# Retention with the decay powers folded into the keys, the mask and the normalisation, and with a block-diagonal state

## What is computed

```python
kc = (k * RET_QK_DIM ** -0.5)          # qc, kc, vc: q, k, v in chunks of c tokens
intra_decay = jnp.where(rel >= 0, jnp.exp(log_gamma[:, None, None] * jnp.maximum(rel, 0.0)), 0.0)
s = jnp.einsum('bnchd,bnshd->bnhcs', qc, kc) * intra_decay
intra = jnp.einsum('bnhcs,bnshe->bnche', s, vc)
k_decay = jnp.exp(log_gamma[:, None] * (CHUNK - 1 - pos)[None, :])
kv = jnp.einsum('bnshd,hs,bnshe->bnhde', kc, k_decay, vc)
def step(state, kv_n):
    return state * chunk_decay + kv_n, state
...
q_decay = jnp.exp(log_gamma[:, None] * (pos + 1.0)[None, :])
cross = jnp.einsum('bnchd,hc,bnhde->bnche', qc, q_decay, prev)
o = head_rmsnorm((intra + cross).reshape(B, S, RET_HEADS, RET_V_DIM))
o = jax.nn.silu(g) * o
```

## Time and profile before

| | us |
|---|---|
| median of 3 runs | 2108.87 (2107.14 to 2109.91) |
| span of the profiled execution | 2105.2 |

### The profile page before, as it was taken

The page is one execution under the profiler, slowest core; times in us unless marked ns, Lnnn a source line. Parts: engine busy times, 40 slices in busy tenths (PEclk is TensorE's granted clock), DMA queues, the critical chain, the costliest instruction groups (busy, mean ns, idle before and its releaser), DMA issues. The chain is left out here.

```text
span 2105.2 us, 30095 instructions
## 1 busy us (share of the span) xinstructions
PE 1959.5 (93%) x11159; PEld 1057.1 (50%) x11159; DVE 1599.9 (76%) x1704; ACT 1056.7 (50%) x1396; POOL 545.7 (26%) x347
## 2 busy tenths in 40 slices
PE   6999988989399999999994899959999999999999
PEld 5785446654244454544443555534544444444444
DVE  6866637753799999999987655484697898889876
ACT  6333327731488888888874555484332333332320
POOL 2222130000133333333320001022003665456530
PEclk9999989999699999999997999979999999999999
DMA  6111410051399999999997446437101112121112
GB/s 245 41 41 41 137 33 1 1 213 60 120 376 413 405 411 410 401 400 404 401 363 273 179 149 233 141 112 264 41 1 61 60 41 80 40 80 40 64 56 80
DMA packets 80627, 363.69 MB, mean 173 GB/s; under 512 B 14088, under 2 KB 27528, under 8 KB 47960
## 3 DMA queue, kind: packets, MB, share of 16 engines
q1 hardware_dynamic: 61704, 309.64, 37.5%
q0 software_dynamic: 18832, 52.80, 7.3%
HBM read 337.21 MB, written 37.75 MB: 178 GB/s over the span
## 5 line engine op out<-in xcount | busy, mean ns | idle before, releaser
L649 DVE SCALAR_TENSOR_TENSOR split<-stage,split 128x2048 f16<-128x2048 f32 x128 | 289.6, 2283 | 5.4 <-ACT split L645 3.6
L432 PE MATMUL ps<-split,xt 128*128 128x512 f16 (+1 forms) x776 | 289.7, 373 | 0.6 <-DVE xt L499 0.6
L433 PE MATMUL ps<-split,xt 128*128 128x512 f16 (+1 forms) x776 | 289.6, 373 | 0.0
L434 PE MATMUL ps<-split,xt 128*128 128x512 f16 (+1 forms) x776 | 289.4, 373 | 0.0
L645 ACT ACTIVATE split<-stage 128x2048 f16<-128x2048 f32 x128 | 240.5, 1904 | 94.6 <-PE ps L434 94.6
L1400 POOL TENSOR_TENSOR stage<-stage 128x1024 f32<-128x1024 f32 x48 | 134.1, 2793 | 266.8 <-DVE split L860 263.9
L432 PE MATMUL ps<-xt,split 128*128 128x512 f16 (+1 forms) x528 | 188.9, 358 | 6.9 <-issue 5.2
L433 PE MATMUL ps<-xt,split 128*128 128x512 f16 (+1 forms) x528 | 189.0, 358 | 0.0
L434 PE MATMUL ps<-xt,split 128*128 128x512 f16 (+1 forms) x528 | 188.9, 358 | 0.0
L649 DVE SCALAR_TENSOR_TENSOR arena<-arena 128x2048 f16<-128x2048 f32 x64 | 146.3, 2286 | 3.1 <-ACT arena L645 3.1
L855 ACT ACTIVATE split<-stage 128x1024 f16<-128x1024 f32 x56 | 57.3, 1048 | 143.2 <-PE pt L434 72.9
(11 more groups left out here) (542 smaller groups left out, 4816.2 us busy)
## 6 DMA issues: line engine op xcount, KB each, us to landing
stage<-in_w_gate SPq DMA_DIRECT2D x64, 1024.0 KB, 7.5
stage<-in_w_up SPq DMA_DIRECT2D x64, 1024.0 KB, 7.8
arena<-in_w_down SPq DMA_DIRECT2D x64, 1024.0 KB, 8.3
stage<-in_w_mlp SPq DMA_DIRECT2D x32, 1024.0 KB, 4.9
stage<-in_w_dense_a SPq DMA_DIRECT2D x16, 1024.0 KB, 8.3
arena<-in_conv_taps POOLq DMA_DIRECT2D x22, 640.0 KB, 4.9
stage<-in_w_dense_b SPq DMA_DIRECT2D x12, 1024.0 KB, 12.0
resid<-in_x SPq DMA_DIRECT2D x16, 512.0 KB, 7.0
```

What stands on the lines that cost most here:

```text
L432: nc.tensor.matmul(out_ap, lh, rh, start=start, stop=False)
L433: nc.tensor.matmul(out_ap, lh, rl, start=False, stop=False)
L434: return nc.tensor.matmul(out_ap, ll, rh, start=False, stop=stop)
L649: nc.vector.scalar_tensor_tensor(out=wlo(s), in0=wstage(s), scalar=WS, in1=whi(s), op0=ALU.mult, op1=ALU.subtract).then_inc(s_wo[s], 1)
```

## The change

Write p for a token's place in its block and g for a head's factor. DVE's reads of the keys from PSUM now multiply by g^(127 - p) / 8 in the same instruction (DVE therefore takes the groups 2, 3, 6, 7, ACT 0, 1, 4, 5). The mask becomes g^-128 on and above the diagonal, and the queries' factor g^(p + 1), constant along a row of the output, moves into the normalisation: as a scale per partition (`rdec`) of ACT's Squares, and as one small product on the reciprocal in `mix`. So qd is gone, and ktok is a plain copy, which ACT now makes (`keys_by_token(n)`, ahead of the statistics of block n - 1 in ACT's order). The state keeps both heads of a pair side by side, 128 x 512, each head's other half zero, in two buffers; DVE zeroes the two PT banks once before the loop. The product with the state is then one matmul of 256 columns for two heads, straight from QR. The products of keys and values come before the waits of the outputs, with a semaphore count of their own, and block 7's transposes and state product, which nobody reads, are gone. The constants c_ret shrink from 1536 to 774 columns. The semaphores' declarations change only in name.

```diff
         onesb = half[:, 6 * P:7 * P]
         ret = Z[:, 0:RET_COLS]
         decT = ret[:, 0:512].rearrange("p (b c) -> p b c", b=2)
-        kdec = ret[:, 512:768]
-        qdec = ret[:, 768:1280].rearrange("p (t j c) -> p t j c", t=2, j=2)
-        cdec = ret[:, 1280:1536]
-        pos = Z[:, RET_COLS:RET_COLS + (S + NH * P) // 2].bitcast(F16)
+        kdec = ret[:, 512:768].rearrange("p (t s) -> p t s", t=2)
+        cdec = ret[:, 768:770]
+        rdec = ret[:, 770:774]
+        pos = Z[:, 1536:1536 + (S + NH * P) // 2].bitcast(F16)
         pos_k = pos[:, 0:S]
         pos_q = pos[:, S:S + NH * P].rearrange("p (h q) -> p h q", h=NH)

...
             return PS[:, 2 * m:2 * m + 2, :].rearrange("p b c -> p (b c)")

         sT = [xn[:, 0, 0:512], xn[:, 0, 512:1024]]
-        qd = [xn[:, 1, 0:512], xn[:, 1, 512:1024]]
-        ktok = [junk[:, 256:512], junk[:, 512:768]]
-        state = junk[:, 0:256]
+        ktok = [xn[:, 1, 0:256], xn[:, 1, 256:512]]
+        state = [junk[:, 0:512], junk[:, 512:1024]]
         zero = cols[:, 42:43]
         lam_in = sq
         lam_dot = cols[:, 64:192].rearrange("p (j d) -> p j d", j=2)
...
                 nc.scalar.activation(chunk_dest(0, ft, tk), PS[:, g % 4, :], ACT.Copy, scale=IWS)\
                     .then_inc(s_free[g % 4], 1)

-            for g in (0, 2, 4):
+            for g in (0, 1, 4):
                 read(g)
             token_hi("T2")
             token_hi("T3")
             proj_hi(act, 1, "S4")
             token_hi("T1")
-            read(6)
+            read(5)
             token_hi("T4")
             proj_hi(act, 1, "S3")
             proj_hi(act, 1, "S1")
...
+            def keys_by_token(n):
+                act.wait_ge(s_rsc, n + 1)
+                if n >= 2:
+                    act.wait_ge(s_lam, 1 + n - 1)
+                nc.scalar.activation(ktok[n % 2], PS[:, 2 * (n % 2), 256:512], ACT.Copy).then_inc(s_sig, 1)
+
+            def out_stats(n):
                 act.wait_ge(s_ro, n + 1)
                 if n:
                     act.wait_ge(s_rmix, n)
                 for h in range(NH):
                     i = nc.scalar.activation(gb[:, h * DV:(h + 1) * DV],
                                              PT[:, 2 + n % 2, h * DV:(h + 1) * DV], ACT.Square,
-                                             accum_out=ss4[:, h:h + 1])
+                                             scale=rdec[:, h:h + 1], accum_out=ss4[:, h:h + 1])
                 ch.done(i)
                 nc.scalar.activation(std4, ss4, ACT.Sqrt, bias=eps, scale=1.0 / DV).then_inc(s_rss, 1)
+
+            for n in range(TT + 1):
+                if n < TT - 1:
+                    keys_by_token(n)
+                if n:
+                    out_stats(n - 1)
             seven(3)
             seven(4)
             for n in (14, 15):
...
             def read(g):
                 dve.wait_ge(s_full[g % 4], g // 4 + 1)
                 _, ft, tk = chunk_groups(0)[g]
-                nc.vector.tensor_scalar(chunk_dest(0, ft, tk), PS[:, g % 4, :], IWS, None, ALU.mult)\
-                    .then_inc(s_free[g % 4], 1)
+                by_block = lambda v: v.rearrange("p (b s) -> p b s", b=4)
+                nc.vector.scalar_tensor_tensor(out=by_block(chunk_dest(0, ft, tk)), in0=by_block(PS[:, g % 4, :]),
+                                               scalar=IWS, in1=kdec[:, ft - 2:ft - 1, :].to_broadcast([P, 4, P]),
+                                               op0=ALU.mult, op1=ALU.mult).then_inc(s_free[g % 4], 1)

             def token_lo(name):
                 n = T_SPLITS.index(name) + 1
...
             dve.wait_ge(s_xl, TT)
-            read(1)
+            dve.wait_ge(s_const, 16 * 8)
+            read(2)
             ch.done(nc.vector.tensor_tensor(TF["T1"], XF[:, 0:4, :], XH[:, 0:4, 0:512], ALU.subtract))
             read(3)
             nc.vector.tensor_tensor(TF["T1"], TF["T1"], XL[:, 0:4, 0:512], ALU.subtract).then_inc(s_hs, 1)
             nc.vector.tensor_tensor(TF["T3"], XF[:, 4:8, :], XF[:, 0:4, :], ALU.subtract).then_inc(s_hs, 1)
             dve.wait_ge(s_hs, 1)
             nc.vector.tensor_tensor(TF["T2"], XF[:, 4:8, :], TF["T1"], ALU.subtract).then_inc(s_hs, 1)
-            read(5)
+            read(6)
             token_lo("T2")
             token_lo("T3")
             proj_lo(dve, 1, "S4")
...
             seven(2)

             def masked(n):
-                par, blk = n % 2, slice(n * P, (n + 1) * P)
+                par = n % 2
                 dve.wait_ge(s_rsc, n + 1)
+                if n < TT - 1:
+                    dve.wait_ge(s_sig, 4 + n + 1)
                 if n >= 2:
                     dve.wait_ge(s_ro, n - 1)
                 nc.vector.tensor_tensor(sT[par].rearrange("p (b c) -> p b c", b=2),
-                                        PS[:, 2 * par:2 * par + 2, 0:256], decT, ALU.mult)
-                nc.vector.tensor_tensor(ktok[par], PS[:, 2 * par, 256:512], kdec, ALU.mult)
-                for t in range(2):
-                    i = nc.vector.tensor_tensor(
-                        qd[par][:, t * 256:t * 256 + 256].rearrange("p (j c) -> p j c", j=2),
-                        QR[:, t:t + 1, blk].to_broadcast([P, 2, P]), qdec[:, t, :, :], ALU.mult)
-                i.then_inc(s_rm, 1)
+                                        PS[:, 2 * par:2 * par + 2, 0:256], decT, ALU.mult).then_inc(s_rm, 1)

             def update(n):
-                dve.wait_ge(s_ro, n + 1)
+                dve.wait_ge(s_lam, 1 + n + 1)
                 if n == 0:
-                    nc.vector.tensor_copy(state, PT[:, n % 2, 256:512]).then_inc(s_rst, 1)
+                    nc.vector.tensor_copy(state[1], PT[:, 0, :]).then_inc(s_rst, 1)
                 else:
-                    ch.done(nc.vector.tensor_tensor(state, state, cdec, ALU.mult))
-                    nc.vector.tensor_tensor(state, PT[:, n % 2, 256:512], state, ALU.add).then_inc(s_rst, 1)
+                    dve.wait_ge(s_ro, n)
+                    dve.wait_ge(s_rst, n + 1)
+                    for t in range(2):
+                        c = slice(2 * t * DV, 2 * (t + 1) * DV)
+                        i = nc.vector.scalar_tensor_tensor(
+                            out=state[(n + 1) % 2][:, c], in0=state[n % 2][:, c], scalar=cdec[:, t:t + 1],
+                            in1=PT[:, n % 2, c], op0=ALU.mult, op1=ALU.add)
+                    i.then_inc(s_rst, 1)

             def mix(n):
                 dve.wait_ge(s_rss, n + 1)
                 ch.done(nc.vector.reciprocal(rst4, std4))
+                ch.done(nc.vector.tensor_tensor(rst4, rst4, rdec, ALU.mult))
                 for h in range(NH):
                     hs = slice(h * DV, (h + 1) * DV)
                     i = nc.vector.scalar_tensor_tensor(
...
                         scalar=rst4[:, h:h + 1], in1=SG[:, n, hs], op0=ALU.mult, op1=ALU.mult)
                 i.then_inc(s_rmix, 1)

+            nc.vector.memset(PT[:, 0, :], 0.0)
+            nc.vector.memset(PT[:, 1, :], 0.0).then_inc(s_rst, 1)
             for n in range(TT + 2):
                 if n < TT:
                     masked(n)
-                if 1 <= n <= TT:
+                if 1 <= n < TT:
                     update(n - 1)
                 if n >= 2:
                     mix(n - 2)
...
                     pe.wait_ge(s_rm, n - 1)
                 for h in range(NH):
                     t, r = h // 2, slice(DH * (h % 2), DH * (h % 2) + DH)
-                    nc.tensor.matmul(PS[:, 2 * par + h % 2, t * P:(t + 1) * P], KR[r, t, blk], QR[r, t, blk],
-                                     start=True, stop=True)
-                for t in range(2):
-                    i = nc.tensor.transpose(PS[:, 2 * par, 256 + t * P:384 + t * P], KR[:, t, blk], ident)
+                    i = nc.tensor.matmul(PS[:, 2 * par + h % 2, t * P:(t + 1) * P], KR[r, t, blk], QR[r, t, blk],
+                                         start=True, stop=True)
+                if n < TT - 1:
+                    for t in range(2):
+                        i = nc.tensor.transpose(PS[:, 2 * par, 256 + t * P:384 + t * P], KR[:, t, blk], ident)
                 i.then_inc(s_rsc, 1)

             def outputs(n):
-                par = n % 2
+                par, blk = n % 2, slice(n * P, (n + 1) * P)
+                if n < TT - 1:
+                    pe.wait_ge(s_sig, 4 + n + 1)
+                    pe.wait_ge(s_rst, max(n, 1))
+                    for h in range(NH):
+                        r0 = DH * (h % 2)
+                        i = nc.tensor.matmul(PT[r0:r0 + DH, par, h * DV:(h + 1) * DV], ktok[par][:, h * DH:(h + 1) * DH],
+                                             VR[:, n, h * DV:(h + 1) * DV], start=True, stop=True)
+                    i.then_inc(s_lam, 1)
                 pe.wait_ge(s_rm, n + 1)
                 if n:
-                    pe.wait_ge(s_rst, n)
-                for h in range(NH):
-                    t, r0 = h // 2, DH * (h % 2)
```

(37 more changed lines are left out.)

## The result

The changed kernel took 2113.69 us (median of 9 runs, 2110.03 to 2115.84), the kernel before 2108.47 beside it (9 runs, 2107.14 to 2111.03). The ratio of the runs is 1.0019, 95% interval 1.001 to 1.0028: about 4 us longer (0.0019 x 2108.47), and within the 0.2% (4.2 us) that was called no change. The forecast was 2112.0.

A forecast was written before the change was run, and what follows sets the result against it. Prediction: a DVE-ACT loop through the key copy bounds the retention, PE outside it; start +0.27, middle +3.68, end -0.78 give +3.2 us, on 2108.87 making 2112.0 us; range 2107 to 2116.5.

The forecast's parts named there:

- The loop: Retention: mix, statistics, key copy, mask product, update, mix run in turn, a round of 5.19 us against 4.27, +0.92.
- The terms: Retention round: the single times, such as Squares' surcharge 0.36, copy 0.40, masked 0.60, update 0.80, mix 1.13, summing to 5.19 us.
- Start: Retention's first blocks, with DVE zeroing two banks: outputs(2) starts at 156.46 instead of 156.19, +0.27 us.
- Middle and end: Retention: outputs(3) to outputs(6) add 4 x 0.92 = +3.68 us; outputs(7), without a key copy, gives -0.78.
- The sign that PE idles 1.4 or more a round: Retention: PE idle 1.4 us or more each round, put down to DVE's mix, would show the forecast right.
- Chunk 0: Reads of chunk 0: swapped groups shift T2's low half and weight splits by +3.2 us, 1.5 of cover remains, no cost.
- The total: Whole kernel: +3.2 on a span of 2105.2, plus 3.7 us between span and median, gives 2112.0, called no change.
- The longer loop: Retention rival: same loop but longer, slower from a round of 5.45 us on, up to 2115.5; chance 0.22.
- S2's weights: Chunk 0 rival: a shift over 4.7 us makes PE stall in `seven(3)`'s counterpart `seven(1)`, 2113.6 at 1.5 beyond; chance 0.05.
- The case of low prices: Retention rival: with terms at their lower bounds rounds take 4.54 us, sum -1.1, 2107.8, no change as well; chance 0.15.
- The PE-bound case: Retention rival: key copies not behind the statistics, four rounds of 3.78 us, -4.2 in all, 2104.7; chance 0.08.
- The rival of a fallen clock: Retention rival: PE's clock falls to 1.2 GHz, its 3.78 us doubles to 7.6 and bounds the round, 2122; chance 0.04.

The follow-up runs named there:

- the experiment with the earlier copy: Changed kernel with ACT copying the keys of block n + 1 ahead of the statistics of block n - 1: 2105.08 us, ratio 0.9987.
- the copy twice: Changed kernel with ACT reading the keys once more, into columns nothing uses, just before each key copy behind the statistics: 2109.36 us, one execution.
- early copy, twice: Changed kernel with the key copies one block earlier, ahead of the statistics, and each made twice by ACT: 2103.74 us, one execution.
- PE filled: Changed kernel with five more matmuls of 128 columns in each outputs(n), into a bank nobody reads at the time: 2111.25 us, ratio 1.0017.
- plain Squares: Changed kernel without the scale column on ACT's Squares, so the sums leave out the rows' decay factor: 2112.03 us, ratio 1.0011.
- two statistics buffers: Changed kernel with two buffers for sums, roots and reciprocals, so statistics of block n wait for mix(n - 2): 2105.93 us, ratio 0.9984.
- copy on DVE, two buffers: Changed kernel with DVE copying the keys and two buffers for the statistics: 2103.89 us, ratio 0.9976.

## Why the prediction was right, step by step

- **The loop: right.** mix, statistics, key copy, mask product, update, mix: 5.19 was the sum, 5.21 is measured. All four tests of it (order, engine, buffers, dose) came out on its side.
- **The terms.** The Squares are 0.37 each, as forecast; with their plain form 0.36 a round is gone. The copy starts 0.20 after the Sqrt and takes 0.36 (0.40 taken). The mask product takes 0.61 to the next start (0.60). The two halves of the update take 0.78 to the reciprocal (0.80). Reciprocal 0.21, the small product 0.19 (0.20 each) and mix 1.13. From the copy's end to the mask product it is 0.09, where 0.03 was taken: this and the shorter copy cancel, so that the sum is within 0.02 is in part luck.
- **The Trainium skill on the Squares' scale** (ScalarE: Activation LUTs, What ACT_TABLE_LOAD costs), that a pointer operand adds about 93 ns to an ACTIVATE: the trace agrees, 0.37 against 0.28, and the plain form shortened the whole round by four times that.
- **Start: right.** outputs(2) was expected at 156.46 and came at 156.79, of which 0.25 had come before the retention. The two zeroings:

```profile
147.29 0.48 DVE L2023 MEMSET pt<- 128x512 f32 x1 [0.18 <-DVE arena L1943]
147.84 0.48 DVE L2024 MEMSET pt<- 128x512 f32 x1
```

 0.55 from start to start (0.60 taken), with 0.18 idle ahead. The estimate from the Trainium skill's rule (VectorE: DVE Perf Modes, Zero memsets can be issued as uint32), 0.53 a bank, was 0.02 off the step and 0.05 off the length. What the zeroing costs the kernel by itself wasn't tried.
- **Middle and end: right.** 181.12 - 177.62 = 3.50 from outputs(6) to outputs(7) (3.49 forecast), and 1.89 for the last outputs (1.89). The sign that PE idles 1.4 or more a round held in four of six rounds; in the other two the low clock took the idle time up. `seven(3)` at 183.01 for 182.6; on PE +3.32 for +3.2.
- **Chunk 0: right, and narrow.** DVE's timeline of the changed kernel:

```profile
65.53 0.69 DVE L1900 SCALAR_TENSOR_TENSOR arena<-ps,zone 128x512 f32<-128x512 f32 x1 [4.53 <-PE ps L433]
66.14 4.49 DVE L1907 TENSOR_TENSOR resid<-arena,resid 128x2048 f16<-128x2048 f32 x2
...
81.21 5.76 DVE L570 SCALAR_TENSOR_TENSOR split<-stage,split 128x1024 f16<-128x1024 f32 x5
```

 DVE waits 4.53 us for group 6. T2's low half begins at 66.14 where it was 62.72, 3.4 later, 0.25 of it from before; the splits run from 81.21. The third of the five ends near 81.21 + 3/5 x 5.76 = 84.7, and PE takes S2 at

```profile
86.23 0.27 PE L431 MATMUL ps<-split,resid 128*128 128x256 f16 x1
```

 without a gap: it is busy 64.00 of 64.00 us from 80 to 144. The cover of about 1.5 us held; what would happen without it wasn't tried.
- **The total: the term that was mis-sized is what lies around the span.** 3.7 us were added as if they lay between span and time. In the changed kernel's profiled execution 2111.01 - 2108.9 = 2.1 lie there, and in the 32 executions of the kernel before beside the first experiments 1.8 to 1.9; the rest was the distance of one execution from the median. In the changed kernel's nine executions it is 1.8 to 3.2, 3.2 in the one whose time is the median; the forecast had no term for that. Medians (+5.2), ratio (about +4.0) and traces (+3.7 on the span) differ by more than the +0.12 by which the walk missed, because single executions scatter by 4 to 10 us. The last section shows what goes with that.

**The rivals.** The longer loop needed 5.45 a round; it is 5.21, though the interval of the ratio (1.001 to 1.0028) reaches past 0.2%. S2's weights came in time. The case of low prices fell with each term measured. The PE-bound case, given 0.08 since only the order in the code spoke against it, is what the experiment with the earlier copy makes of the kernel: rounds of 3.55 (3.78 worked out), and against the kernel before -3.3 us by the medians, -2.7 by the ratio and -4.00 in the retention (30.87 for 34.87), where -4.2 was the price. The rival of a fallen clock (0.04) was half right, and this is the one step in which its reasoning missed: the granted clock did fall,

```profile
167.60:171.00 3.40, 3.40 (x16) 2.91 (x16) 1.62 (x5) 1.63 (x9) 0.00 (x0) 0.50 0.00 0
177.80:181.20 3.40, 3.40 (x13) 2.83 (x12) 2.52 (x9) 1.57 (x9) 0.00 (x0) 0.50 0.01 2
```

for two stretches of 3.4 us in which PE's work takes twice as long, level 1.2 GHz, after rounds with 1.4 us or more of idle time each. That it would then bind the loop was wrong, but narrowly. It doesn't last, and in 3.4 us at half speed PE loses 1.7 us of work (an estimate), about the 1.6 to 2.0 us that it idles otherwise. PE reached outputs(5) and outputs(7) without any idle time, just as the mix let it go:

```profile
179.85 1.12 DVE L2018 SCALAR_TENSOR_TENSOR arena<-pt,cols,arena 128x128 f32<-128x128 f32 x4
```

The mix ends at 180.97 and outputs(7) begins at 181.12, 0.15 later, the same distance as where PE idles (160.72 + 1.13 and 162.00). So no time was lost, but no slack was left.

**Better than both.** With the copy on DVE just ahead of the mask product the kernel takes 2103.90 us, 0.9977 (0.9967 to 0.9987) of the kernel before. The lighter computation, with the copy on DVE, was worth 34.87 - 29.80 = 5.07 us of retention all along; the place of one 0.36 us copy turned it into +3.32.

## What to carry to other kernels

Before a small step is moved to an engine with time to spare, look at what stands ahead of it in that engine's order and whether that waits, even a block back, for the engine that will wait for the step: an idle share is no cover if both sit in one loop. Follow the loop around with start-to-start times, one term for each handover; here eleven terms of a trace that had never run the new order met the round to 0.02 us, two misses of 0.04 and 0.06 cancelling. To prove such a loop, change the order without the work, and add work inside and outside of it: in the loop nearly all of it showed (1.28 of 1.35 us), outside less than a third (0.55 of 1.8).

## What the runs showed of the hardware

**A low granted clock of PE can cost nothing, as long as the idle time lasts.** In the retention PE ran twice 3.4 us at 0.50 of full speed; holding it at 1.00 by filling its idle time left the rounds at 5.21. But the low stretches used the slack up: PE's idle time of 1.6 to 2.0 us a round was 0 in these two. In the kernel with the copy twice, whose rounds are 5.48, it fell twice as well, and PE's idle time before the next outputs was 0.23 and 0.65 instead of 1.88. No run has a longer low stretch in the retention.

**Executions differ in the later stages too, and the difference goes with the clock.** From `seven(3)` to the end of the span all ten kernels run the same code. In their profiled executions it takes 1924.3 to 1932.6 us, and it is longer where the granted clock is low for longer after the retention (from the trace's clock records):

```
kernel                       rest (us)   of it at the low clock (us)
the copy twice                1924.3       99.0
before                        1925.8      116.1
changed                       1925.9      109.2
early copy, twice             1925.9      109.2
copy ahead of statistics      1927.3      116.1
PE filled                     1927.9      109.2
plain Squares                 1929.1      116.1
two statistics buffers        1929.3      116.1
copy on DVE                   1931.3      119.5
copy on DVE, two buffers      1932.6      122.9
```

The correlation is 0.82. Executions of one and the same kernel show it too: over the 32 of the kernel before beside the first experiments, spans of 2104.1 to 2111.2 us and the mean granted clock of each correlate with -0.77 (0.975 in the two shortest). The ends in the windows view, the copy twice and then copy on DVE with two buffers:

```profile
183.19:2107.50 1924.31, 1798.18 (x9873) 926.00 (x9870) 1467.39 (x1531) 979.24 (x1253) 511.49 (x330) 0.97 0.47 180
```

```profile
174.98:2107.60 1932.62, 1806.21 (x9873) 931.30 (x9870) 1469.03 (x1529) 979.77 (x1253) 511.43 (x330) 0.97 0.47 179
```

The same counts of PE's instructions, 8 us more. One of the places, in the latter and in the kernel before:

```profile
1163.00:1293.00 130.00, 123.09 (x860) 71.29 (x858) 71.03 (x97) 67.13 (x114) 8.60 (x16) 0.96 0.54 199
```

```profile
1165.90:1295.90 130.00, 124.24 (x892) 71.91 (x891) 72.11 (x98) 68.27 (x115) 8.64 (x16) 1.00 0.55 201
```

860 matmuls at a clock of 0.96 against 892 at 1.00 in the same 130 us. One execution of each kernel can't say whether the clock's fall is the cause or follows a wait, nor whether it depends on when the retention ends; that stays open. A scatter of this size would hide that two versions are 0.83 us apart on the trace, and it is why the length of the changed stage, with the same end points in each trace, was the sharper measure here.
